# A two-block transformer on one core: every split activation gets another address, modulo 256 bytes, against its weights

## The reference

```python
proj = h @ w_in                                   # layers 0, 1: 1024 x 7168
y_r = retention_branch(q, k, v, g) @ w_ret        # the operand r
x = x + g2 * ((gelu(a) * b) @ w_down)             # the operand u, 2816 wide
y = gp * (pool_o @ w_po) + gs * (sgu_o @ w_so) + ga * (attn_o @ w_ao)   # operands b
h = h + g2 * (jnp.square(jax.nn.relu(h @ w1)) @ w2)                     # the operand f, 4096 wide
```

## The kernel before, in words

| operand | layers | before | after |
|---|---|---|---|
| h | 0, 1, 2, 3 | -64, -64, 0, -64 | -32, +32, -128, +96 |
| u | 0, 1 | -64, -64 | -48, -80 |
| r | 0, 1 | -64, -64 | 0, 0 |
| b | 2, 3 | 0, -64 | +96, -112 |
| f | 2, 3 | 0, -64 | +32, -16 |

## Time and profile before

### The profile page before, as it was taken

How to read it: one execution, slowest core, us unless ns; L and a number is a source line. 1 busy time by engine, 2 the same in 40 slices (tenths; PEclk the granted TensorE clock), 3 DMA queues, 4 the chain that set the end, 5 groups by cost and what they waited for, 6 DMA issues and landing times.

```text
span 2096.8 us, 36942 instructions
## 1 busy us (share of the span) xinstructions
PE 2053.7 (98%) x14236; PEld 1888.9 (90%) x14236; DVE 1503.1 (72%) x2161; ACT 986.1 (47%) x1501; POOL 394.0 (19%) x288
## 2 busy tenths in 40 slices
PE   8999999999999999999999999999999989999998
PEld 7999999999999999999877888988888988899998
DVE  5876889986777899988988524898533375866554
ACT  3444456645444565654245433432143154855553
POOL 0330203310511212314201002121020031121120
PEclk8999999999999999999999999999999999999999
DMA  7776767786675666664554323366633243755553
GB/s 285 288 261 201 258 216 247 246 296 210 224 241 193 219 201 195 216 223 141 191 171 141 106 85 98 105 199 220 199 111 101 71 161 125 248 201 167 196 193 109
DMA packets 109594, 396.36 MB, mean 189 GB/s; under 512 B 12408, under 2 KB 13056, under 8 KB 109056
## 3 DMA queue, kind: packets, MB, share of 16 engines
q1 hardware_dynamic: 108160, 389.99, 55.0%
q0 software_dynamic: 1280, 4.20, 0.6%
HBM read 393.09 MB, written 1.05 MB: 188 GB/s over the span
## 4 chain that ended last, share of the span: by engine, by line
PE 83%; DVE 12%; ACT 2%; DMA 2%; issue 1%; POOL 1%; DVEq 0%; SPq 0%; ACTq 0%; POOLq 0%
PE bank L499 21%; PE bank L500 20%; PE bank L501 20%; DVE w_lo L1448 5%; PE bank L598 2%; PE bank L599 2%; PE bank L600 2%; DVE stage L1469 2%; DMA stage<-in_stream 1%; PE bank L671 1%; PE bank L674 1%; DVE rstd L1466 1%; PE bank L619 1%; PE bank L523 1%; PE bank L522 1%
## 5 line engine op out<-in xcount | busy, mean ns | idle before, releaser
L1448 DVE TENSOR_TENSOR w_lo<-stage,w_hi 128x1024 fp32r<-128x1024 f32 x536 | 708.8, 1337 | 434.9 <-ACT w_hi L1017 433.6
L1017 ACT ACTIVATE w_hi<-stage 128x1024 fp32r<-128x1024 f32 x536 | 565.2, 1059 | 836.9 <-PE bank L501 568.0
L499 PE MATMUL bank<-h_hi,w_hi 128*128 128x256 f32 (+1 forms) x2560 | 782.5, 306 | 12.6 <-DVE w_lo L1448 8.1
L500 PE MATMUL bank<-h_lo,w_hi 128*128 128x256 f32 (+1 forms) x2560 | 776.4, 303 | 0.0
L501 PE MATMUL bank<-h_hi,w_lo 128*128 128x256 f32 (+1 forms) x2560 | 776.3, 303 | 0.0
L499 PEld LDWEIGHTS bank<-h_hi,w_hi 128*128 128x128 f32 x2560 | 484.1, 189 | 42.8 <-DVE w_lo L1448 12.5
L501 PEld LDWEIGHTS bank<-h_hi,w_lo 128*128 128x128 f32 x2560 | 486.9, 190 | 21.6
L500 PEld LDWEIGHTS bank<-h_lo,w_hi 128*128 128x128 f32 x2560 | 483.6, 189 | 21.8 <-issue 0.5
L1469 DVE SCALAR_TENSOR_TENSOR stage<-stage,cvec 128x1024 f32<-128x1024 f32 x188 | 257.0, 1368 | 3.4 <-DMA stage<-in_stream 1.0
L499 PE MATMUL bank<-f_hi,w_hi 128*128 128x256 f32 (+1 forms) x448 | 145.3, 324 | 0.0
L500 PE MATMUL bank<-f_lo,w_hi 128*128 128x256 f32 (+1 forms) x448 | 145.3, 324 | 0.0
(11 more groups left out here) (254 smaller groups left out, 3247.4 us busy)
## 6 DMA issues: line engine op xcount, KB each, us to landing
stage<-in_stream SPq DMA_DIRECT2D x728, 512.0 KB, 4.3
bias<-in_bias POOLq DMA_DIRECT2D x16, 256.0 KB, 3.2
X<-in_x SPq DMA_DIRECT2D x2, 1024.0 KB, 6.7
cvec<-in_cvec SPq DMA_DIRECT2D x3, 512.0 KB, 4.4
decay<-in_decay SPq DMA_DIRECT2D x1, 1024.0 KB, 6.0
out<-X SPq DMA_DIRECT2D x4, 256.0 KB, 2.0
rope<-in_rope SPq DMA_DIRECT2D x2, 256.0 KB, 4.7
wsgu<-in_wsgu SPq DMA_DIRECT2D x2, 256.0 KB
```

The lines of the kernel that those rows point to most:

```text
L499: mm(out, w_hi[:, slot, w], xh[:, c, 0:T], start=first, stop=False)
L500: mm(out, w_hi[:, slot, w], xl[:, c, 0:T], start=False, stop=False)
L1017: A(w_hi[:, m % NR, :], stage[:, n % NS, :], ACT.Copy).then_inc(hi_ready, 1)
L1448: do(V.tensor_tensor(w_lo[:, m % NR, :], stage[:, n % NS, :], w_hi[:, m % NR, :].bitcast(F32), ALU.subtract), unit_done, done_value(n))
```

## The change

It gives new addresses to the split activations, and moves nothing else in the program: the sequence of instructions and waits of each engine is the same as before. Tiles are allocated at multiples of 32 bytes, so for offsets in between, `operands` now allocates a slightly longer flat tile and uses it from some columns on.

```diff
         def operands(name, shape, at):
-            tiles = {a: sb(name if n == 0 else f"{name}_{n}", shape, F32R, a) for n, a in enumerate(sorted(set(at)))}
+            tiles = {}
+            for n, a in enumerate(sorted(set(at))):
+                past = a % 32
+                flat = sb(name if n == 0 else f"{name}_{n}", [P, shape[1] * shape[2] + past // 4], F32R, a - past)
+                tiles[a] = flat[:, past // 4:].rearrange("p (c t) -> p c t", c=shape[1])
             return [tiles[a] for a in at]
...
-        h_at = [edge + off for off in (448, 448, 512, 448)]
+        h_at = [edge + off for off in (480, 544, 640, 608)]
...
-        ph = where[0] + 64
-        top = ph + 64
+        ph = where[0] + 0
+        top = ph + 96
...
-        u_at = [ph + off for off in (0, 0)]
+        u_at = [ph + off for off in (208, 176)]
...
-        b_at = [ph + 40 * KB + off for off in (0, 0, 64, 0)]
+        b_at = [ph + 40 * KB + off for off in (0, 0, 96, 144)]
...
-        f_at = [ph + off for off in (0, 0, 64, 0)]
+        f_at = [ph + off for off in (0, 0, 32, 240)]
```

## The result

The changed kernel takes 2129.8 us (median of 4, 2128.1 to 2131.5) against 2099.6, a ratio of 1.0144 with a 95% interval of 1.0120 to 1.0168. I had forecast 2095, no change, with a range to 2128 and 0.22 for slower by over 1%. The rival whose time came about is "more collisions", which I had put at 2130.

A forecast was written before the change was run, and what follows sets the result against it. TensorE's matmul pace was taken to bound the kernel. Terms -9.1 + 1.7 - 3.1 + 5.8 + 2.6 gave -2.1 us against a profiled 2098.63, 1.2 us over the median 2097.4: 2095 us, range 2068 to 2128.

The forecast's parts named there:

- more collisions: Rival: at the new distances weight loads meet matmul reads each pass; two thirds of 47.6 us, 2130 us; chance 0.25.
- What bounds the kernel: Whole kernel: TensorE, busy 98%, bounds it; its pace depends on the distance between weight load and matmul reads.
- The two patterns at -64: 256 columns at distance -64: record means of 276 or 281 ns, nothing between in a steady stretch.
- r to 0: r in layers 0 and 1, moved to distance 0: 283 ns means, +1.7 us.
- 256 columns in layer 2: Layer 2, moved to -128 and +32: 690 matmuls from 7 to 2.5 ns, -3.1 us; bounds -4.8 and 0.
- h and u in layers 0 and 1: Moved to -32, +32, -48, -80: 2.5 ns each, 13.6 us against 22.7, -9.1; bounds 0 to 38.0.
- 22.7 us of excess now: h and u, layers 0 and 1, before the change: what their record means have over 276 ns, totalled.
- 512 columns in layer 2: Layer 2, moved to -128, +32, +96: 2304 matmuls at 2.5 ns, +5.8 us; bounds 0 to 16.1.
- Layer 3: h to +96, b to -112, f to -16: 4.0 us becomes 6.6, +2.6; bounds -4.0 and +14.5.
- Token blocks: Blocks with activations as stationary operand: means 388 to 394 ns, some 1 us of excess; no term in the sum.
- My signs: Lines by form: r 283, layer 2's 512 columns over 389, layer 3's f over 276; collisions: h means 283 or above.
- below today's best: Rival: at a right distance matmuls run at 107 and 213 ns, under any pace seen; about 2030 us; chance 0.03.

The follow-up runs named there:

- table1: Matmuls alone, no part of the model, at 16 distances and two widths, after two kinds of start; 113.3 to 120.0 ns at 256 columns, 226.7 to 236.7 at 512.

## Why the prediction was wrong, step by step

- **What bounds the kernel** was right: TensorE's pace, set by distance and width; rest moved by only 3.5 us. The two patterns at -64 were right as well.
- **r to 0**: forecast +1.7 us, measured +1.7 (0.8 to 2.5 us of added time).
- **256 columns in layer 2**: forecast -3.1, measured -1.8 (6.8 to 5.0); right in sign.
- **h and u in layers 0 and 1**: forecast -9.1, measured +9.1 (15.9 to 25.0). This is half of the miss. (The base varies: the second profile of the kernel before has 14.0 instead of 15.9.) I had read 22.7 us of excess now from means that also hold the matmuls after a stall, and gave the unknown distances 2.5 ns each; they have 116.7 to 119.2 ns, 3.3 to 5.9 over the floor.
- **512 columns in layer 2**: forecast +5.8, measured +13.0. The value was 6.7 ns from start to start (in the means 393 to 395 against 389), near the upper bound of 7. My thought that half of 256 bytes "may change nothing" was wrong: -128 gives 233.4.
- **Layer 3**: forecast +2.6, measured +12.9 (2.1 to 15.0), with `h` at +96 at 120.0, as bad as 0. `f` at -16, which I had called the likeliest loser, has 3.8 ns for each matmul, the least of the three (`b` 5.1, `h` 6.6), and 2.9 us in all; `h` has 9.6.
- Token blocks, which I had left at no change, added 2 us.

The step that failed is one: "I take 2.5, the middle of the two patterns (0 and 5) seen off distance zero, since the rows at -64 are nearest", and the same 2.5 in the other terms. The runs showed 3.3 to 6.7 ns in its place. Near in bytes says nothing here. -64 is one of very few low points among 64 distances whose mean is 119.2 ns, 5.9 over the floor, and the rows of before probably show it because somebody had picked it.

The rival "more collisions" came about from the point that I had named, a mean excess of 5 ns: measured were 64.6 us over 12,694 starts, 5.1 ns each. That its 2130 us came out to the microsecond is luck. Its bounds were rightly taken from the rows, but the "two thirds" had no reason; of its four parts, priced in full at 15.3, 1.7, 16.1 and 14.5 us, 9.1, 1.7, 13.0 and 12.9 came, and less waiting, the gain in layer 2 and the token blocks made up the difference. It deserved the higher chance.

My signs didn't tell the cases apart. `r` at 283, the 512 columns over 389 and layer 3's `f` over 276 all came, as they would under "more collisions" too, and the mean of the larger group of `h` at 256 columns in layer 2 stayed at 283. The sign of that rival, means of 283 in the `h` rows, came in layer 3 alone (284, one over my bound); in layers 0 and 1 the means of `h` stood still at 281 and 280 while its added time rose by 6.6 us. A mean that mixes steady stretches with the matmuls after a stall is too blunt for 2 ns.

On the rule of the Trainium skill, "SBUF — State Buffer", section "Who interferes with whom", that only the shared port pair contends: with TensorE alone in table1 the pace still ranges from 113.3 to 120.0 ns by distance. That section also calls TensorE's two read ports independent, and gives no reason for a pace that goes by distance; the measurement decides. That the two streams of reads hinder each other is my reading of it. The pace "below today's best" did not appear at any of 64 distances.

## What to carry to other kernels

When the trace shows a quantity at only the values that somebody chose, and its other values are unknown, price them by the bounds and lean to the bad end; a chosen value is no sample of the rest. A pace of matmuls is read from start to start, not from busy time, and a table of it costs one short kernel: the 88 blocks of table1, 1460 us in all, told more than any argument. And where one program runs at two paces, compare profiles of the same program before attributing a difference to a change.

## What the runs showed of the hardware

- The time from one fp32r matmul to the next, each with its own weight load, depends on the distance of activations and weights modulo 256 bytes and on the width: 113.3 to 126.7 ns for 256 columns and 226.7 to 240.0 for 512, at a granted clock of 1.00. A shift of both operands, tried at four distances, changed nothing beyond switching between two patterns.
- The best distance for 256 columns (+112, or -64 after some starts) is a poor one for 512 (231 to 233 ns), and the best for 512 (0) is poor for 256 (120.0).
- At -64 with 256 columns two patterns, 113.3 and 117.8 ns, mostly last until the next interruption, and the same program can have either in the same stretch. One matmul with an odd distance is felt for three or four matmuls there; with 512 columns at 0 and at +112 one in eight can change all eight.
- Steps of 4 bytes matter: 113.5 at +112, 121.6 at +116. Why the values come in this order stays open.
